# Expert weights taken by pairs of column chunks, down weights issued from ScalarE's queue, tokens turned by VectorE, routing regrouped

## The reference

```
h = rmsnorm(x, ffn_norm[1])                      # (256, 1024)
logits = h @ router                              # 8 experts
top_val, top_idx = top_k(logits, 2); gates = softmax(top_val)
for each expert e, for the tokens that chose e:
    hid = silu(xb @ w_gate[e]) * (xb @ w_up[e])  # 1024 -> 3584
    y[tokens] += (hid @ w_down[e]) * gate        # 3584 -> 1024
x = x + y;  out = rmsnorm(x, final_norm)
```

## Time and profile before

| what | us |
|---|---|
| median of 3 runs | 1459.54 (1459.48 to 1459.99) |
| the profiled execution's own time | 1458.45 |
| its span (first to last instruction) | 1456.7 |
| TensorE busy | 1443.4 |
| VectorE busy | 1198.4 |
| ScalarE busy | 972.6 |
| GpSimd busy | 122.5 |

### The profile page before, as it was taken

How to read it: one execution, slowest core, us unless ns; L and a number is a source line. 1 busy time by engine, 2 the same in 40 slices (tenths; PEclk the granted TensorE clock), 3 DMA queues, 4 the chain that set the end, 5 groups by cost and what they waited for, 6 DMA issues and landing times.

```text
span 1456.7 us, 20213 instructions
## 1 busy us (share of the span) xinstructions
PE 1443.4 (99%) x7493; PEld 1215.3 (83%) x7493; DVE 1198.4 (82%) x978; ACT 972.6 (67%) x894; POOL 122.5 (8%) x139
## 2 busy tenths in 40 slices
PE   9999999999999999999999999999999999999998
PEld 8988888888988888888888888888888888888886
DVE  5876766666877788888888888888888888888897
ACT  5556544445465577777777777777777777777775
POOL 5312000000312450000000000000000000000200
PEclk9999999999999999999999999999999999999999
DMA  8634976562533599999999999999999999999994
GB/s 256 227 118 143 352 255 207 168 203 73 174 116 116 195 402 393 393 392 394 378 369 394 378 369 397 377 377 384 382 371 377 393 376 373 394 375 363 399 394 165
DMA packets 210282, 450.23 MB, mean 309 GB/s; under 512 B 12940, under 2 KB 37048, under 8 KB 210232
## 3 DMA queue, kind: packets, MB, share of 16 engines
q1 hardware_dynamic: 208936, 445.09, 83.9%
q0 software_dynamic: 1152, 4.19, 0.7%
q10 hardware_dynamic: 144, 0.26, 0.0%
HBM read 435.36 MB, written 14.16 MB: 309 GB/s over the span
## 4 chain that ended last, share of the span: by engine, by line
PE 97%; ACT 1%; DVE 1%; issue 0%; POOL 0%; DVEq 0%; POOLq 0%
PE bank L1737 27%; PE bank L1739 26%; PE bank L1738 26%; PE bank L2191 5%; PE bank L2193 3%; PE bank L2240 2%; PE bank L1897 1%; PE bank L1744 1%; PE bank L1966 0%; PE bank L1937 0%; PE bank L2228 0%; PE bank L1757 0%; ACT XN L939 0%; ACT winh L911 0%; PE bank L2218 0%; DVE winl L1227 0%
## 5 line engine op out<-in xcount | busy, mean ns | idle before, releaser
L1221 DVE TENSOR_TENSOR low<-raw,high 128x2048 fp32r<-128x2048 f32 x336 | 766.8, 2291 | 103.4 <-ACT high L1122 102.6
L1122 ACT CAST high<-raw 128x2048 fp32r<-128x2048 f32 x335 | 642.1, 1917 | 179.7 <-PE bank L1739 179.7
L1737 PE MATMUL bank<-high,xeh 128*128 128x512 f32 x896 | 353.6, 395 | 0.0
L1739 PE MATMUL bank<-high,xel 128*128 128x512 f32 x896 | 349.6, 390 | 0.0
L1738 PE MATMUL bank<-low,xeh 128*128 128x512 f32 x896 | 348.9, 389 | 0.0
L1739 PEld LDWEIGHTS bank<-high,xel 128*128 128x128 f32 x896 | 168.2, 188 | 35.8
L1738 PEld LDWEIGHTS bank<-low,xeh 128*128 128x128 f32 x896 | 168.5, 188 | 33.8
L1737 PEld LDWEIGHTS bank<-high,xeh 128*128 128x128 f32 x896 | 168.3, 188 | 33.9 <-issue 0.4
L1737 PE MATMUL bank<-high,hdh 128*128 128x512 f32 x444 | 173.5, 391 | 0.0
L1739 PE MATMUL bank<-high,hdl 128*128 128x512 f32 x444 | 172.9, 389 | 0.0
L1738 PE MATMUL bank<-low,hdh 128*128 128x512 f32 x444 | 172.8, 389 | 0.0
(11 more groups left out here) (378 smaller groups left out, 1848.8 us busy)
## 6 DMA issues: line engine op xcount, KB each, us to landing
raw<-in_moe_w_gate_dram SPq DMA_DIRECT2D x112, 1024.0 KB, 7.5
raw<-in_moe_w_up_dram SPq DMA_DIRECT2D x112, 1024.0 KB, 7.7
raw<-in_moe_w_down_dram SPq DMA_DIRECT2D x112, 1024.0 KB, 7.5
ring<-in_w_in_dram SPq DMA_DIRECT2D x10, 2048.0 KB
dring<-in_dense_w_gate_dram SPq DMA_DIRECT2D x5, 2048.0 KB
dring<-in_dense_w_up_dram SPq DMA_DIRECT2D x5, 2048.0 KB
dring<-in_dense_w_down_dram SPq DMA_DIRECT2D x5, 2048.0 KB
ring<-in_w_in_dram SPq DMA_DIRECT2D x8, 1024.0 KB, 8.6
```

Source lines behind the costliest of these rows:

```text
L1122: act.copy(high[:, q % SPLIT, :], raw[:, q % RAW, :]).then_inc(s_hi, 1)
L1221: dve.tensor_tensor(low[:, q % SPLIT, :], raw[:, q % RAW, :], high[:, q % SPLIT, :].bitcast(F32), ALU.subtract).then_inc(s_lo, 1)
L1737: pe.matmul(o, xh, wh, start=first, stop=False)
L1739: return pe.matmul(o, xl, wh, start=False, stop=last)
```

## The change

- **Order of the pieces.** Chunks go in pairs (0,1), (2,3), (4,5) and 6 alone (`GROUPS`). A gate or up piece of a pair is two blocks of 128 rows by 1024 columns, so rows of 4 KB, and feeds two PSUM banks. A pair has four gate pieces, then two down pieces of the pair before, four up pieces, two more down pieces. Both silus of a pair follow one another on ScalarE, both multiplications on VectorE. `hid` of the two chunks is turned after the first and the second piece of the next group (`TURNED`: pieces 8, 9, 20, 21, 32, 33; the last chunk still at 39).
- **Down weights** are issued by ScalarE (`load_down`), each before the cast five pieces ahead of it, after the same wait on VectorE as before; the other 28 pieces of a job by SP.
- **Tokens.** ScalarE rewrites the rows of `XN` by blocks of 32 columns (`rows_by_quadrant`, two copies of 1024 columns, in job 0) and GpSimd scatters these. SP reads a job's tokens with four transfers of 32 rows, which exchange the 32x32 blocks, and VectorE turns within the blocks with one instruction of 1024 columns (`turn_tokens`, after piece 33). TensorE turns no tokens any more.
- **Routing.** The cast of piece 0 moves from GpSimd to ScalarE. The transposes of the first 128 tokens' x come before the last 12 matmuls of the output projection; those of the second 128 and the router's products alternate; one unread matmul goes between the two halves of these products and six (before four) behind them. VectorE prepares tokens and pieces 1 and 2 of job 0 before it computes the job list, and the list takes fewer steps. Job 0 is written out ahead of the loops, so nobody waits for the list before job 0.

The core of the diff (line numbers of what is kept are those of the kernel before; parts that only rename are left out):

```diff
-    ORDER = []
-    for c in range(NCH):
-        ORDER += [("gate", c, 0), ("gate", c, 1), ("up", c, 0), ("up", c, 1)]
-        if c:
-            ORDER += [("down", c - 1, 0), ("down", c - 1, 1)]
-    ORDER += [("down", NCH - 1, 0), ("down", NCH - 1, 1)]
+    GROUPS = [tuple(range(c, min(c + 2, NCH))) for c in range(0, NCH, 2)]
+
+    def products(kind, group):
+        return [(kind, group[0], h) for h in range(2 * len(group))]
+
+    def downs(c):
+        return [("down", c, h) for h in range(2)]
+
+    ORDER, TURNED = [], {}
+    for i, group in enumerate(GROUPS):
+        done = GROUPS[i - 1] if i else ()
+        for c in done:
+            TURNED[len(ORDER) + c - done[0]] = c
+        ORDER += products("gate", group) + (downs(done[0]) if done else [])
+        ORDER += products("up", group) + (downs(done[1]) if done else [])
+    ORDER += downs(NCH - 1)
+    group_of = {group[0]: group for group in GROUPS}
+
+    def ends(q, what):
+        kind, c, h = ORDER[q]
+        return kind == what and h == 2 * len(group_of[c]) - 1
+
...
+    GAP_DENSE, GAP_COPY, GAP_CHOICE = 6, 1, 6
...
+                    if q == TOKENS_AT and before is None:
                         if isinstance(j, int):
                             sp.wait_ge(s_sent, 16 * 2 * T)
-                        sp.wait_ge(s_gx, 2 * j + 2)
-                        sp.dma_start(tokens[:, :], routed[bass.ds(j + 2, 1), :, :].rearrange("o p d -> p (o d)"))\
-                            .then_inc(s_tok, 16)
-                    if q >= RAW or not isinstance(j, int):
+                            sp.wait_ge(s_gx, 2)
+                        else:
+                            sp.wait_ge(s_tt, j)
+                        for b in range(QUADS):
+                            v = slice(b * D // QUADS, (b + 1) * D // QUADS)
+                            sp.dma_start(tokens[b * SQUARE:(b + 1) * SQUARE, :].rearrange("i (a n) -> i a n", a=QUADS),
+                                         routed[bass.ds(j + 2, 1), :, v].rearrange("o (a i) n -> i (o a) n", i=SQUARE))\
+                                .then_inc(s_tok, 16)
+                    if kind == "down":
+                        continue
+                    if before is not None and q < RAW:
+                        sp.wait_ge(s_lo, nth_piece(before, NPC + q - RAW))
+                    elif q >= RAW or not isinstance(j, int):
                         sp.wait_ge(s_lo, nth_piece(j, q - RAW))
...
             job(0, 0)
             sp.wait_ge(s_jl, 1)
-            njobs = sp.value_load(jobs[0:1, 16:17], min_val=2, max_val=MAXJOBS)
-            with sp.Fori(1, njobs) as j:
...
+            with sp.Fori(1, last) as j:
                 e = sp.value_load(jobs[0:1, bass.ds(j, 1)], min_val=0, max_val=NE - 1)
...
-                    if i == 2 * DEPTH - 1 and t == 0:
-                        pool.wait_ge(raw_loaded[0], 16)
-                        pool.wait_ge(s_wil, NCAST * DEPTH)
-                        pool.tensor_copy(high[:, 0, :], raw[:, 0, :]).then_inc(s_hi, 1)
...
-                                            XN[:, t, :], None).then_inc(s_sent, 16)
+                                            gathered[:, 0, t, :], None).then_inc(s_sent, 16)
...
+                    act.wait_ge(raw_loaded[0], 16)
+                    act.wait_ge(s_wil, NCAST * DEPTH)
+                    act.copy(high[:, 0, :], raw[:, 0, :]).then_inc(s_hi, 1)
+                    square_sum(2 * l + 1, 1, 0)
+                    turned_copy(2 * l + 1, dst, 1, 0)
...
+                if not (isinstance(j, int) and j == 0):
+                    act.wait_ge(s_tt, j)
+                    act.wait_ge(s_used, nth_use(j - 1, AT["up", NCH - 1, 1]))
...
+            def rows_by_quadrant(t):
+
+                act.copy(gathered[:, 0, t, :].rearrange("p (b k j) -> p k b j", b=QUADS, k=KD),
+                         XN[:, t, :].rearrange("p (k b j) -> p k b j", b=QUADS, k=KD)).then_inc(s_rx, 1)
...
-            def job(j, is_last=False):
+            def load_down(j, e, q):
+
+                kind, c, h = ORDER[q]
+                if kind != "down":
+                    return
+                r = ECH[c][0] + h * BANK // 2
+                act.wait_ge(s_lo, nth_piece(j, q - RAW))
+                act.dma_start(raw[:, q % RAW, :].rearrange("p (k n) -> p k n", n=D),
+                              moe_w_down[0, bass.ds(e, 1), r:r + BANK // 2, :].rearrange("o (k p) n -> p (o k) n", p=P))\
+                    .then_inc(raw_loaded[q % RAW], 16)
...
                 for q in range(SPLIT, NPC):
+                    if q + RAW - 2 < NPC:
+                        load_down(j, e, q + RAW - 2)
...
+                    if isinstance(j, int) and q - SPLIT < T:
+                        rows_by_quadrant(q - SPLIT)
...
-                    if ORDER[p][0] == "gate" and ORDER[p][2] == 1:
-                        c = ORDER[p][1]
+                    if ends(p, "gate"):
                         act.wait_ge(s_used, nth_use(j, p))
-                        if c >= 2:
-                            act.wait_ge(s_eh, NCH * j + c - 1)
...
+                        for c in group_of[ORDER[p][1]]:
+                            if c >= 2:
+                                act.wait_ge(s_eh, NCH * j + c - 1)
+                            act.activation(sil[:, c % 2, :], ps[c % 2][:, :], ACT.Silu).then_inc(s_es, 1)
+                    if p in TURNED:
+                        c = TURNED[p]
+                        act.wait_ge(s_et, NCH * j + c + 1)
+                        act.copy(hdh[:, c % 2, :], ps[6][:, :]).then_inc(s_hh, 1)
...
-            with act.Fori(0, last) as j:
-                job(j)
-            job(last, is_last=True)
+            job(0, 0)
+            act.wait_ge(s_jl, 1)
+            last = act.value_load(jobs[0:1, 17:18], min_val=1, max_val=MAXJOBS - 1)
+            with act.Fori(1, last) as j:
+                job(j, act.value_load(jobs[0:1, bass.ds(j, 1)], min_val=0, max_val=NE - 1))
...
+            def turn_tokens(j):
+
+                dve.wait_ge(s_tok, 16 * QUADS * j)
+                dve.wait_ge(s_xl, 2 * j)
+                dve.transpose(tokens_T[:, :, :].rearrange("p k (a i) -> p a k i", a=QUADS),
+                              tokens[:, :].rearrange("p (a k j) -> p a k j", a=QUADS, k=KD)).then_inc(s_tt, 1)
...
             dve.tensor_copy(row(11), rank).then_inc(s_rank, 1)
+            tokens_low(0, (0,))
+            piece_low(0, 1)
+            tokens_low(0, (1,))
+            piece_low(0, 2)
             dve.wait_ge(s_rk, 2)
...
-            by_job(JB[:, 2, :], cidx[:, 1, :])
+            over = OH[:, 0, 0:16 * NE].rearrange("p (j e) -> p j e", e=NE)
+            last_job = JB[:, 1, :].rearrange("p (e b) -> p e b", b=2)[:, :, 1]
+            then(dve.tensor_tensor(over, bc(last_job.unsqueeze(1), [P, 16, NE]), bc(cidx[:, :].unsqueeze(2), [P, 16, NE]), ALU.is_lt))
+            then(dve.tensor_reduce(JB[:, 2, :], over, AX.X, ALU.add))
             then(dve.tensor_copy(jobs[:, 0:16], JB[:, 2, :]))
...
+                    if q == SQUARES_AT and not is_last:
+                        turn_tokens(j + 1)
...
-                    if ORDER[p][2] == 1:
-                        kind, c, _ = ORDER[p]
-                        if kind == "gate" and c:
-                            hidden_low(j, c - 1)
-                        if kind == "up":
+                    if p in TURNED:
+                        hidden_low(j, TURNED[p])
+                    if ends(p, "up"):
+                        dve.wait_ge(s_used, nth_use(j, p))
+                        for c in group_of[ORDER[p][1]]:
                             dve.wait_ge(s_es, NCH * j + c + 1)
-                            dve.wait_ge(s_used, nth_use(j, p))
...
-                for n in range(2) if l else (1,):
-                    turn(2 * l + 1, 0, n)
+                    if l and not n:
+                        for m in range(2):
+                            turn(2 * l + 1, 0, m)
...
                     pe.matmul(ps[0][:, 0:2], ident[:, :], UO[:, 0:2], start=True, stop=True).then_inc(s_used, SPLIT)
                     for n in range(2):
                         turn(2 * l + 1, 1, n)
-                    router_logits(0)
+                        router_logits(0, (n,))
+                    keep_running(0, GAP_COPY)
...
-            keep_running(4, GAP_CHOICE)
+            keep_running(0, GAP_CHOICE)
...
-            def turn_tokens(j):
...
             gather()
-            pe.wait_ge(s_jl, 1)
-            last = pe.value_load(jobs[0:1, 17:18], min_val=1, max_val=MAXJOBS - 1)
...
-                        if not is_last:
-                            turn_tokens(j + 1)
...
+                        m = len(group_of[c])
+                        for r in range(4 // m):
+                            k = 4 // m * h + r
+                            for i in range(m):
+                                w = slice((m * r + i) * BANK, (m * r + i + 1) * BANK)
```

(39 more changed lines are left out.)

106 lines of the change are left out of this document (45 added, 61 removed).

## The result

The changed kernel takes **1464.69 us** (median of 8 runs, 1462.31 to 1467.61), the kernel before 1459.78 beside it (8 runs, 1458.62 to 1459.99). The ratio is 1.0036 with a 95% interval of 1.0027 to 1.0044, so it is slower by more than the 0.2% that can be told. Its runs also lie further apart, 5.3 us where those of the kernel before lie 1.4 apart. The profiled execution took 1465.27, its span is 1463.5.

What follows compares the result with a forecast made beforehand. TensorE bounds the expert stage, with VectorE and ScalarE close behind. Terms -6.1 + 3.1 + 0.7 + 1.9 - 1.8 + 0.4 = -1.8 us give 1457.7 us against the median; range 1450.5 to 1470.

Steps and rivals of the forecast that it cites:

- rival 3: VectorE's token transposition takes twice as long, holding up the second turn by 1.1 us more: slower, 1465.3 us; chance 0.12.
- Two queues and 4 KB rows: Weight transfers: SP has time to issue and TensorE never waits for them, so worth 0 in both signs.
- Routing: Before job 0: the changed order of small products keeps the clock, so job 0 starts 1.8 us earlier.
- rival 4: Routing: the clock falls all the same, the 1.8 us is missing, 1459.5 to 1460.2 us; chance 0.08.
- Tokens off TensorE: Eight token transposes leave TensorE, saving 0.87 us in each of seven jobs: -6.1 us.
- Border: Between two jobs, TensorE waits 0.27 us for the next job's first subtraction, seven times: +1.9 us.
- Two silus: Second silu delays the next cast; TensorE waits at pieces 6, 14 and 26, 0.39 us a job: +3.1 us.
- The transposition: VectorE turns tokens between pieces 33 and 34; TensorE waits 0.1 us at the second turn, seven times: +0.7 us.
- The job list: VectorE's list of jobs now stands ahead of piece 3's subtraction in job 0: +0.4 us.
- Rival 2: ScalarE's issues hold up casts at pieces 14, 26 and 36; at 1.0 us each, 1469.7 us; chance 0.13.

Runs made afterwards that it cites:

- experiment 1: Changed kernel with every down piece issued by SP again in its place of the order; pairs, tokens and routing stay as changed: 1460.05 us, ratio 1.0002.
- chunks_tokens_early: Changed kernel with one queue, chunk-by-chunk order, and the first half of the next job's tokens cast and subtracted early, behind piece 40: 1453.18 us, ratio 0.9953.
- run 9: Two versions: alternating queues with two of four token reads issued by ScalarE, 1465.86 us; changed kernel with all four issued by ScalarE, 1485.41 us.
- run 3: Kernel before, its order, routing and TensorE transposes untouched, with the down pieces issued by ScalarE: 1468.62 us, ratio 1.0057.
- 8: Changed kernel with pieces alternating between two queues from piece 9 on, ScalarE issuing odd and SP even ones: 1466.34 us, ratio 1.0053.
- tokens_with_downs: Changed kernel with all four token reads of a job issued by ScalarE, in the queue of the down pieces: 1485.41 us, ratio 1.0166.

## Why the prediction was wrong, point by point

The direction was wrong. The time lies in the range, but near the 1465.3 of rival 3 by chance only: none of the named mechanisms made it.

- **The step that failed: "Two queues and 4 KB rows. Worth 0 in both signs."** It costs 4.6 us by the medians with and without (1464.69, 1460.05), 5.0 by their ratios (1.0036, 1.0002). I argued from TensorE never waiting and from SP being short of no time. Both were true of one queue, and neither speaks of order. The row I used holds half of what I left out: the DMA share is 1.04, so the DMA engines are hardly ever idle. The other half I had not asked for: a piece in the kernel before takes 11.6 us from issue to landing in job 0 (4.9 at best, the row in experiment 1). Nobody waits, because the line is served in the order of need. A second line breaks that order. The Trainium skill, "DMA: Bandwidth & Descriptors", section "Queues, rings and completion order", says that each DMA engine takes turns between the queues that have work, a packet at a time; by that rule a piece of the short queue overtakes, and the trace agrees: 52.8% and 51.1% of the DMA engines' time for the two queues, landings of 8.9 beside 15.5 us. I did not weigh that rule.
- **Routing, -1.8: failed in most executions.** The mean granted clock of the span is 0.999 in one of the eight (1462.31 us, the fastest) and 0.995 to 0.997 in the rest. In the profiled one the clock fell to 0.50 and job 0 began at 498.24, 0.3 later than before. Where it stays at 1.00 (run 1), job 0 begins at 496.28, and I had 496.1. The size was right; that the new order keeps the clock was rival 4's point, and it does not reliably.
- **Tokens off TensorE, -0.87 a job: right.** With its covers repaired (`chunks_tokens_early`) a job takes 117.69 instead of 118.51, 0.82 less.
- **Border, +0.27 a job: right.** 0.18 of lateness and 0.11 more at the matmul behind it (the rows at 738.67).
- **Two silus, +0.39 a job: right in sum, wrong in make-up.** At pieces 6, 14 and 26 TensorE is 0.02 late where I had 0.11 to 0.14, and the matmul behind the wait costs 0.11 more, in each, which I had missed. Two errors cancel, by luck. Of the 0.14, 0.03 was for an issue that costs nothing there: it runs beside the second silu, and the cast starts 0.97 behind the first one, where the two silus alone were to give 0.98.

```profile
772.80 0.60 ACT L1207 ACTIVATE sil<-bank 128x512 f32<-128x512 f32 x1 [0.80 <-PE bank L1799]
772.94 0.38 ACTq L1182 DMA_DIRECT2D raw<-in_moe_w_down_dram  x1
773.30 0.59 ACT L1207 ACTIVATE sil<-bank 128x512 f32<-128x512 f32 x1
773.77 3.71 ACT L1160 CAST high<-raw 128x2048 fp32r<-128x2048 f32 x2
```

- **The transposition, 1.21 us and 0.1 of waiting: right.** The trace has 1.236, and 0.04 of lateness at the turn in an undisturbed job. Rival 3 falls, and with it the estimate of 2.49 us by the page of the Trainium skill.

```profile
L1644 DVE STREAM_TRANSPOSE tokens_turned<-tokens_results x7: 1235/1236/1239, 593.2 to 1303.8; 128x1024 f32<-128x1024 f32 x7
```

- **The job list, +0.4: right.** TensorE is 0.39 late at 506.91.
- **Rival 2, ScalarE's issues: not in the change, but real.** 0.38 each, hidden; two or four token reads more at the same place, and it decides (run 9). SP's queue, which I took to hold seven transfers, holds four or five in job 0 of the kernel before.

So the forecast for jobs 1 to 6 was -0.11 each and the trace says -0.06. Of seven terms two were wrong, and they were the two in which the profile's rows do not give a duration: the order in which transfers are served, and the clock. 4.6 and, where the clock falls, 1.8 are 6.4 of the 7.0 us between the forecast 1457.7 and the measured 1464.69.

**What stays open.** Why the clock falls in some executions and not in others of one routing code; why TensorE waited at four places of the last job in one execution of the change and at one in another; what a version with two queues would take if ScalarE had room for its issues, which was not tried; and how much of the overtaking is due to the rows being of unequal length in run 3 (4 KB for down pieces, 2 KB for the others), where the loss was largest.

## What to carry to other kernels

Before work goes to a second DMA queue, read the DMA share and the time from issue to landing, stage by stage. The share alone does not tell: it is 1.03 both in job 0 and from 620 to 1380 us of the kernel before, and the change cost job 0 3.3 us and jobs 1 to 6 nothing. Where a piece also takes far longer to land than at best (11.6 and 12.6 us in the first and last job, 7.4 between, 4.9 at best), the queue is the schedule: pieces arrive in the order of need because they stand in one line, and a shorter line beside it overtakes, though bytes and rate are the same. Gains from taking work off the bounding engine come whole only after the covers that this work gave to other chains are rebuilt: here half of the tokens' casts and subtractions, moved by one piece, was worth 3.1 us by the medians (1456.31, 1453.18) and 1.9 by seven jobs of 0.27. And a trace of one execution can't say that a clock will be kept; look at two before a term is put on it.

## What had not been expected of the hardware

- Behind even a short wait TensorE's first matmul of 512 columns takes 0.34 to the next start instead of 0.23 (738.67 to 739.01).
- In the expert stage, behind five idle times of TensorE of 1.98 to 2.71 us (runs 3, 8 and `tokens_with_downs`), some eight matmuls ran at a granted clock of 0.50; behind six of 1.63 to 1.79 none did.
- Two queues with work in both each got half of the DMA engines' time (52.8 and 51.1% from 1414 to 1425.5 us of the changed kernel).
- VectorE turns a 128x1024 float32 tile within its 32x32 blocks in 1.24 us, no longer than an elementwise pass of that width would take by the neighbouring rows.
